# Gated recurrence on one Trainium2 core: the 64 sample tokens taken into the seven-product scheme, halves of 288 columns

## The reference

```
q, f, i, g = split(x @ w_in, 4)            # x: 576 tokens x 1024, each of q, f, i, g: 16 heads x 128
k, logf = from sigmoid(f) and a lower bound; q = silu(q); v = i
S = exp(b_end) * S + (k * exp(b_end - b))^T v                # per head, chunk by chunk
o = att(q, k, decay) v + (q * exp(b)) S                      # b: running sum of logf
y = rms_norm(o) * silu(g) @ w_out ; x = layer_norm(alpha * x + y)
```

## Time and profile before

| | |
|---|---|
| three runs | 2052.65, 2060.71, 2062.13 us (median 2060.71) |
| span of the profiled execution | 2054.1 us |
| the profiled execution's own time | not among the data shown; its span lies 6.6 us below the median and 1.5 us above the lowest run |
| busy: PE, DVE, ACT, POOL | 1953.3, 1045.5, 770.9, 384.4 us |
| the recurrence in the span | from 1274 to about 1940 us |
| mean granted TensorE clock | 0.980 |

### The profile page before, as it was taken

The page is one execution under the profiler, slowest core; times in us unless marked ns, Lnnn a source line. Parts: engine busy times, 40 slices in busy tenths (PEclk is TensorE's granted clock), DMA queues, the critical chain, the costliest instruction groups (busy, mean ns, idle before and its releaser), DMA issues. The chain is left out here.

```text
span 2054.1 us, 46521 instructions
## 1 busy us (share of the span) xinstructions
PE 1953.3 (95%) x19082; PEld 1465.8 (71%) x19082; DVE 1045.5 (51%) x2629; ACT 770.9 (38%) x1683; POOL 384.4 (19%) x424
## 2 busy tenths in 40 slices
PE   7999999989997999997999899899999999999998
PEld 7888888866666778875666344687888778788543
DVE  3111131148874443434766233678777777877332
ACT  0000011158873444433677001355445544544300
POOL 5432333335660000003452100000000000000000
PEclk9999999999998999998999999999999999999999
DMA  6333322444149999997564923599998998998730
GB/s 181 100 124 93 81 66 72 82 94 152 51 161 288 379 380 380 392 371 274 193 241 152 269 67 106 177 282 313 323 312 267 324 302 275 307 313 300 231 133 26
DMA packets 222098, 443.39 MB, mean 216 GB/s; under 512 B 60832, under 2 KB 182193, under 8 KB 205249
## 3 DMA queue, kind: packets, MB, share of 16 engines
q1 hardware_dynamic: 214432, 364.57, 55.4%
q0 software_dynamic: 7456, 75.86, 10.1%
HBM read 413.70 MB, written 165.23 MB: 282 GB/s over the span
## 5 line engine op out<-in xcount | busy, mean ns | idle before, releaser
L2315 PE MATMUL three<-x1T,arena 128*128 128x256 f32 x768 | 204.1, 393 | 0.9 <-DVE rec_qq L2706 0.9
L580 POOL TENSOR_TENSOR late<-late 128x512 f32<-128x512 f32 (+2 forms) x76 | 112.1, 1476 | 220.9 <-PE pab_bZ L368 127.7
L2614 POOL TENSOR_TENSOR rec_v_own<-rec_rows,row_own 64x512 f32<-64x512 f32 x16 | 16.5, 1032 | 717.9 <-PE rec_bX L2429 593.3
L2315 PEld LDWEIGHTS three<-x1T,arena 128*128 128x128 f32 x768 | 135.3, 190 | 15.4 <-DVE rec_qq L2706 1.3
L852 ACT ACTIVATE ap_sc<-ap_sc,ap_nmax 128x256 f32<-128x256 f32 (+1 forms) x192 | 106.3, 557 | 2.4 <-DVE ap_nmax L876 2.3
L1477 DVE COPY sa_kT<-sa_bT 128x512 f32<-128x512 f32 x80 | 55.2, 690 | 94.9 <-PE sa_bT L1333 94.8
L876 DVE CUSTOM_DVE_ANT_0 ap_sc<-ap_bS,ap_bias 128x256 f32<-128x256 f32 (+1 forms) x192 | 86.1, 486 | 12.0 <-DMA ap_bias<-in_bias_p 7.4
L1477 ACT COPY sa_kT<-sa_bT 128x512 f32<-128x512 f32 x80 | 46.9, 586 | 99.0 <-PE sa_bT L1333 98.8
L911 POOL TENSOR_SCALAR ap_sc<-ap_sc,ap_rden,sgl 128x256 f32<-128x256 f32 (+3 forms) x128 | 76.4, 607 | 40.4 <-DVE ap_rden L884 40.2
L1496 DVE COPY sa_xT<-sa_bT 128x512 f32<-128x512 f32 x64 | 43.8, 684 | 66.4 <-PE sa_bT L1398 66.1
L1333 PE MATMUL sa_bT<-ident,arena 64*128 64x64 f32 x1280 | 58.5, 231 | 14.2 <-issue 4.8
(11 more groups left out here) (513 smaller groups left out, 4567.4 us busy)
## 6 DMA issues: line engine op xcount, KB each, us to landing
out<-in_cache_a_k SPq DMA_DIRECT2D x8, 8160.0 KB, 29.6
out<-in_cache_a_v SPq DMA_DIRECT2D x8, 8160.0 KB, 29.4
arena<-in_cache_a_k SPq DMA_DIRECT2D x40, 1024.0 KB, 8.7
arena<-in_cache_a_v SPq DMA_DIRECT2D x40, 1024.0 KB, 9.0
arena<-in_w_in_c SPq DMA_DIRECT2D x64, 512.0 KB, 6.8
late<-in_w_in_ab SPq DMA_DIRECT2D x128, 64.0 KB, 2.4
late<-in_w_in_ab SPq DMA_DIRECT2D x8, 1024.0 KB, 5.4
ap_bias<-in_bias_p SPq DMA_DIRECT2D x16, 512.0 KB, 4.0
```

The lines of the kernel that those rows point to most:

```text
L580: nc.gpsimd.tensor_tensor(to, a, b, op).then_inc(sums, 1)
L2315: last = nc.tensor.matmul(bank[:, 0:SEQ // 2], left[:, k, :], right[:, k, :], start=(first and k == 0), stop=(k == 3), skip_group_check=True)
```

## The change

The token halves become 288 columns wide and hold the samples too. Tokens are dealt to the two halves in groups of 32 (`GROUP`): each half is nine groups of 32, at a distance of 64. All 576 tokens go through the scheme.

- `product` is four matmuls of 288 columns; the moving operand is nine runs of 32 columns where it is read straight from the tokens (B11 to B22), and contiguous for T1, T2, T4. Copies and adds are 288 wide and write nine runs.
- `project_rows`, `turn_side` and ACT's copies of `rows` and `side` are gone, and so are its separate exponential and SiLUs of the samples: the one for all 576 columns does it.
- The sample values come out of `vT` by a fifth transpose in `turn_values`, into `bS`, and ACT copies them to `sV`; GpSimd's `v_own` now waits for that copy (`v_read`).
- `turn_values(h - 1)` moves behind product 1 of head `h`, and ACT's copy of the values behind copy 0.
- T4 is made after B12 rather than before it, and several buffers change places.
- Nothing changes in DVE's order of adds, exponents, scale, sums and finish, and no DMA is added or taken away.

The core of the diff:

```diff
-        T1, T2 = (x.rearrange("p (k t) -> p k t", k=4) for x in spare[0:2])
-        T4 = s.sb("T4", [P, 4, SEQ // 2])
+        GROUP, NT_HALF = 32, TOK // 2
+        def half(a, which):
+            return a.rearrange("p (g two c) -> p g two c", two=2, c=GROUP)[:, :, which, :]
+        def grouped(a):
+            return a.rearrange("p (g c) -> p g c", c=GROUP)
...
-                def project_rows(h):
-                    pe.wait_ge(w_ready[h % 2], 64 * (h // 2) + 64)
...
-                    for k in range(KD):
-                        for half in range(2):
-                            last = nc.tensor.matmul(bS[TS * half:TS * half + TS, 0:2 * P], xT[:, k, SEQ:TOK],
-                                                    w[h % 2][:, 2 * half:2 * half + 2, k, :], start=(k == 0), stop=(k == KD - 1))
-                    last.then_inc(rows_done, 1)
...
-                        last = nc.tensor.matmul(bank[:, 0:SEQ // 2], left[:, k, :], right[:, k, :], start=(first and k == 0), stop=(k == 3),
-                                                skip_group_check=True)
+                        last = nc.tensor.matmul(grouped(bank[:, 0:NT_HALF]), left[:, k, :], right[:, k, :, :], start=(first and k == 0),
+                                                stop=(k == 3), skip_group_check=True)
...
                     product(A11, B11, bR[0], True)
-                    side()
+                    values_before()
                     pe.wait_ge(summed, SUMS * h + 1)
                     pe.wait_ge(tokens, 1)
                     product(S1, T1, bR[2], True)
...
-                        last = nc.tensor.transpose(bO[:, m * P:(m + 1) * P], vT[:, m * P:(m + 1) * P], ident[:, :])
-                    last.then_inc(v_done, 1)
+                        nc.tensor.transpose(bO[:, m * P:(m + 1) * P], vT[:, m * P:(m + 1) * P], ident[:, :])
+                    nc.tensor.transpose(bS[0:TS, P:2 * P], vT[:, SEQ:TOK], ident[:, :]).then_inc(v_done, 1)
...
-                    nc.scalar.copy(to, bR[0][:, 0:SEQ // 2]).then_inc(copied, 1)
+                    nc.scalar.copy(to, grouped(bR[0][:, 0:NT_HALF])).then_inc(copied, 1)
...
-                    pool.wait_ge(rows_ready, h + 1)
+                    pool.wait_ge(v_read, h + 1)
...
-                    nc.vector.tensor_tensor(out, bank[:, 0:SEQ // 2], more, ALU.add).then_inc(added, 1)
+                    nc.vector.tensor_tensor(out, grouped(bank[:, 0:NT_HALF]), more, ALU.add).then_inc(added, 1)
```

More of the change, by code:

```diff
@@ L2197, in recurrence, with token_sum, weight_sum @@
         tmp = near
-        T1, T2 = (x.rearrange("p (k t) -> p k t", k=4) for x in spare[0:2])
-        T4 = s.sb("T4", [P, 4, SEQ // 2])
-        SUM = [[s.sb(f"S{i}", [P, 4, P]) for i in (1, 2, 4)],
[L2201 to L2205, removed]
+        GROUP, NT_HALF = 32, TOK // 2
[3 more added lines that the diff above has]
+            return a.rearrange("p (g c) -> p g c", c=GROUP)
+        def token_sum(a):
+            return a.rearrange("p (k g c) -> p k g c", k=4, c=GROUP)
+        def weight_sum(a):
+            return a.rearrange("p (k c) -> p k c", k=4)
+        early, late = spare[:, 0:2 * D_MODEL], spare[:, 2 * D_MODEL:4 * D_MODEL]
+        T1, T4 = token_sum(early[:, 0:4 * NT_HALF]), token_sum(late[:, 0:4 * NT_HALF])
+        T2 = token_sum(s.sb("T2", [P, 4 * NT_HALF])[:, :])
+        SUM = [[s.sb(f"S{i}", [P, 4, P]) for i in (1, 2, 4)],
+               [weight_sum(x[:, 4 * NT_HALF:4 * NT_HALF + 512]) for x in (early, late)] + [s.sb("S4_second", [P, 4, P])]]
+        vT = s.sb("vT", [P, TOK])
+        (B11, B12), (B21, B22) = ([xT[:, 4 * k:4 * k + 4, :].rearrange("p k (g two c) -> p k g two c", two=2, c=GROUP)[:, :, :, which, :]
+                                   for which in range(2)] for k in range(2))
         q_near, k_near, k_end = (s.sb(n, [P, TOK]) for n in ("q_near", "k_near", "k_end"))
@@ L2220, in recurrence @@
         bS, bA, bU, bO, bX = (s.bank(n) for n in ("bS", "bA", "bU", "bO", "bX"))
-        rows = [s.sb(f"rows{u}", [P, 2 * P]) for u in range(2)]
-        sV = [r[0:TS, 0:P] for r in rows]
-        side = [s.sb(f"side{u}", [P, 3 * TS]) for u in range(2)]
+        sV = s.sb("sV", [TS, P])
         V_AT, Q_AT, F_AT, G_AT = range(4)
@@ L2342, in forget_and_queries @@
                     pe.wait_ge(summed, SUMS * h + 7)
-                    pe.wait_ge(tokens, 4)
+                    pe.wait_ge(tokens, 3)
                     pe.wait_ge(copied, COPIES * h + 2)
@@ L2346, in forget_and_queries @@
                     updates_before()
+                    pe.wait_ge(tokens, 4)
                     pe.wait_ge(added, ADDS * h + 4)
@@ L2447, in own_pairs @@
                     pe.wait_ge(st0_ready[h % 2], 16 * (h // 2) + 16)
-                    if h + 1 < HC:
-                        pe.wait_ge(side_read, h + 2)
-                    nc.tensor.matmul(bS[:, 0:TS], sV[h % 2], att_s[:, :], start=True, stop=True)
+                    pe.wait_ge(v_read, h + 1)
+                    if h >= 1:
+                        pe.wait_ge(os_copied, h)
+                    nc.tensor.matmul(bS[:, 0:TS], sV[:, :], att_s[:, :], start=True, stop=True)
                 def own_state(h, b):
@@ L2529, in _ @@
                     if before:
[L2530 to L2533, removed]
+                        if h >= 1:
+                            act.wait_ge(k_ready, h)
+                        copy(h, 0, half(sf[:, :], 1))
+                        if h == 0:
+                            act.wait_ge(lb_ready, 1)
+                            nc.scalar.activation(lb[:, :], one_lb[:, :], ACT.Exp).then_inc(lb_ready, 1)
                     if behind:
@@ L2537, in _ @@
                             act.wait_ge(o_done, h - 1)
-                        nc.scalar.copy(v[:, :, :].rearrange("p m v -> p (m v)"), bO[:, :]).then_inc(v_read, 1)
+                            act.wait_ge(os_done, h - 1)
+                            act.wait_ge(own_ready, h - 1)
+                        nc.scalar.copy(v[:, :, :].rearrange("p m v -> p (m v)"), bO[:, :])
+                        nc.scalar.copy(sV[:, :], bS[0:TS, P:2 * P]).then_inc(v_read, 1)
                     if before:
                         if h >= 1:
[L2541 to L2550, removed]
                             act.wait_ge(far_ready, h)
-                        copy(h, 1, qq[:, 0:SEQ // 2])
+                        copy(h, 1, half(qq[:, :], 0))
                     if behind:
@@ L2559, in _ @@
                         act.wait_ge(added, ADDS * h + 3)
-                        nc.scalar.activation(sf[:, 0:SEQ], sf[:, 0:SEQ], ACT.Exp, scale=-1.0).then_inc(f_read, 1)
+                        nc.scalar.activation(sf[:, :], sf[:, :], ACT.Exp, scale=-1.0).then_inc(f_read, 1)
                     if behind:
@@ L2564, in _ @@
                         act.wait_ge(added, ADDS * h + 5)
-                        nc.scalar.activation(qq[:, 0:SEQ], qq[:, 0:SEQ], ACT.Silu).then_inc(q_read, 1)
-                        nc.scalar.activation(qq[:, SEQ:TOK], side[h % 2][:, TS:2 * TS], ACT.Silu).then_inc(q_ready, 1)
-                        copy(h, 2, vT[:, SEQ // 2:SEQ])
+                        nc.scalar.activation(qq[:, :], qq[:, :], ACT.Silu).then_inc(q_ready, 1)
+                        copy(h, 2, half(vT[:, :], 1))
                         act.wait_ge(fg_ready, h + 1)
@@ L2575, in _ @@
                             act.wait_ge(out_ready, h - 1)
-                        copy(h, 3, gg[h % 2][:, 0:SEQ // 2])
+                        copy(h, 3, half(gg[h % 2][:, :], 0))
                     if behind:
@@ L2793, in _ @@
                         dve.wait_ge(copied, COPIES * h + 2)
-                        add(h, 1, 2, bR[2], qq[:, T_2], qq[:, T_1])
-                        add(h, 2, 4, bR[1], sf[:, T_1], sf[:, T_2])
+                        add(h, 1, 2, bR[2], half(qq[:, :], 1), half(qq[:, :], 0))
+                        add(h, 2, 4, bR[1], half(sf[:, :], 0), half(sf[:, :], 1))
                     if behind:
```

65 lines of the change are left out of this document (24 added, 41 removed).

## The result

The changed kernel takes 2112.66 us (median of four runs, 2110.99 to 2116.24) against 2059.19 us for the kernel before beside it: ratio 1.026, 95% interval 1.024 to 1.028. That is +53.5 us, slower, inside the range, against a forecast of +64. A second set of runs, in the last experiment, gave 2116.60 us and 1.027 (1.025 to 1.030). One run, of the kernel with the values turned first, was in a slow state (2313.11 us at a granted clock of 0.83) and is left out of its median.

A forecast was written before the change was run, and what follows sets the result against it. PE looked busiest, but DVE's chain to S1 was taken as nearly as late and holding product 2. From 2060.7 us, +40 without clock falls and +24 for falls made +64, 2125 us; range 2095 to 2152 us.

The forecast's parts named there:

- DVE is nearly as late as PE: Before product 2, PE arrives only 0.33 us after DVE's sum S1, which product 2 needs.
- stretch one: From the end of product 9 to the start of product 2: +0.67 us, with PE's saving turned into 3.9 us idle.
- stretch two: From product 2 to the end of product 9: PE sets the pace, eight wider products add 1.73 us.
- rival 5: In product's moving operand, breaks between the nine runs cost 14 ns each: +100 us, about 2200 us; chance 0.07.
- rival 4: In the products, weight loads or issue set the pace, so 288 columns cost what 256 do: 2063 us; chance 0.05.
- Rival 3: In the rounds, S1 is ready in time and PE stays the bound: 1.47 us less each, 2043 us; chance 0.08.
- The term of 24 us: PE's clock falls in 7 of 15 rounds, each 6.8 us at half speed, losing 3.4 us: +24 us.
- Rival 1: In heads 1 to 15 PE's clock holds despite the idle gaps: 2101 us; chance 0.23.
- Rival 2: PE's clock falls in every round: +91 us, 2152 us; chance 0.12.
- The ends: Outside the repeated rounds: head 0 costs about +4 us, the last round's end 2.8 us.
- The sum without the clock: Whole kernel without clock falls: 4 for head 0, 14 x 2.40 for rounds, 2.8 at the end, +40 us.
- product 5's margin: Before product 5, 1.9 us + 0.3 of slack covers the 0.76 us that GpSimd's v_own adds to DVE's sums.

The follow-up runs named there:

- the last experiment: Changed kernel with the values turned ahead of product 1 again: 2127.73 us, 1.033; the changed kernel ran again beside it, 2116.60 us, 1.027.
- the extra sum: One unused 512-column DVE sum added ahead of S1: before kernel 2063.39 us, changed kernel 2136.34 us, changed kernel with idle-time matmuls 2108.62 us.
- the filled kernel: Changed kernel with four idle-time matmuls a head on PE, results never read: 2098.92 us, 1.019.
- the fastest one: Changed kernel with DVE's sums made early, products 1 and 2 swapped, and ACT's copy 0 ahead of the norm's exponential: 2041.78 us, 0.992.

## Why the prediction was right

**The bound.** The step "DVE is nearly as late as PE" was right and carried everything. Its slack was forecast as 0.33 us by the rows. It came out as 0.28 at product 2 and 0.17 for the whole round by the extra sum; the start behind a wait, 0.10 us, had no term in the forecast. S1's end moved from 18.71 to 19.66 us behind copy 2, +0.95 against 0.96 forecast. Removing 4.60 us of PE work and wait from stretch one gained nothing; it became idle, 1.15 + 0.79 + 1.50 = 3.44 us against 3.9 forecast.

**The size of a round.** Forecast +2.40 us, measured +2.49: stretch one +0.68 (forecast 0.67), stretch two the rest, +1.81 (forecast 1.73), and 0.10 of that is product 2's start behind its wait. The nine runs cost nothing, so rival 5 is out. The pace went up with the columns, which takes rival 4 out. Rival 3, PE stays the bound, is refuted for this kernel but was a true description of what lay behind the waits: with three edits of order, on DVE, PE and ACT, the round falls to 38.49.

**The clock.** Here two sizes were off, and they partly cancel. The number of rounds that hold a fall was put at 7 and is 10, nine of them at a cost. The price was taken from a stretch with 6.8 us at half clock, 3.4 us lost; in these rounds a fall is 3.4 us long and costs 1.5 to 1.7, so that they are 43.9 us long and not 45.5. The term of 24 us should have been 15, and this is most of why +64 was forecast and +53.5 measured. Which rounds hold a fall stays open. Rival 1 (the clock holds) did not come true, but the filled kernel shows its size, 2098.9 us against 2101. Rival 2 appears in the kernels with the extra sum or the values first, not in the change. By the second failure mode in the Trainium skill's page TensorE: Matmul & The Clock Gate, brief idling between groups makes the clock swing; the trace agrees, in ten rounds of 15.

**The ends.** Head 0 was put at +4 us to S1 of head 1 and came to +2.8. PE's first work in the recurrence starts at 1279.84 after and 1274.57 before, S1 of head 1 at 1325.73 and 1317.65. Up to product 5 it is -0.2, as forecast. The wait ahead of product 5 is 4.12 us (forecast 4.8), and one fall lies behind it, of 3.4 us, which loses 1.7 us where 2.5 were forecast:

```profile
1294.42 3.56 PE L2315 MATMUL three<-x1T,rec_S 128*128 128x288 f32 x8 [4.12 <-DVE rec_qq L2693]
```

From S1 of head 15 to the end of the span it is +2.9, against 2.8 forecast. The sum without the clock is then 2.8 + 14 x 2.49 + 2.9 = 40.6 us, against 40.

The first two starts also say that 5.3 us of the profile's 60.3 come from ahead of the recurrence, in code that the change doesn't touch; the medians, 53.5 apart, are the better measure.

**GpSimd beside DVE.** The third sum takes 1.50 us instead of 0.69, which the step priced at 0.76 and hid behind product 5's margin. By the Trainium skill (SBUF — State Buffer, two separate sides) this lock was to be expected in each head; the trace agrees, with one of these sums at 1.50 or 1.51 us in each of the 15 rounds. Product 5 (1637.62) still comes well after add 1 (1635.43). In the kernel before, `v_own` ran beside DVE's reciprocal, which reads one tensor (1609.36 to 1613.11, `v_own` from 1610.60), and that took 3.75 us, as it does in the changed kernel with nothing beside it.

## What to carry to other kernels

An engine that is busy for 98% of the time can have a second chain 0.2 us behind it; ask of each piece of work that is taken away which other engine's instruction the next consumer also waits for. Idle time on PE can cost more than its length: here three waits of 3.44 us in all brought falls of the clock worth another 15 us, and useless matmuls in the gaps took them away. Where a saving vanishes, look for the next waits one after the other and move the producers to where their engines idle or are free; here three changes of order turned +53 us into -18.

## What the runs showed of the hardware that I had not expected

- Falls of the clock come in more than one length. At the start of the recurrence it was 6.8 us at 1.2 GHz in the changed kernel (13.7 in the fastest one), in its rounds 3.4 us, in six rounds with the values turned first 6.8.
- A fall costs only where PE sets the pace: up to 1.69 us in nine rounds, nothing in the first, where PE waited for S1 behind it.
- In the round whose rows are shown first PE was busy for 2.91 of 5.5 us (1623.0 to 1628.5), and the clock stayed at 2.4 GHz, as in four others; nearly the same gaps brought a fall in nine. One wait of 4.12 us in place of three brought a fall in all 15 rounds.
- A product that starts behind a wait takes 0.10 us longer to the start of the next one.
- 0.60 us more on DVE lengthened the rounds by 0.60 us with the gaps filled. With them open it also took the falls from 10 rounds to 15.
- In the trace, a wait for several semaphores was put down to a DVE sum that ended 0.04 us after the copy that was really waited for; only the run with the copy moved told them apart.
